# Matrix memory's scores and numerators as three fp32r products each, in a two-layer mixer block

## The reference

```
s[t,u]  = (q[t] . k[u]) * exp(decay of gates from u to t)      u before or at t
num[t]  = sum_u s[t,u] * v[u]
den[t]  = sum_u s[t,u]
h[t]    = num[t] / max(|den[t]|, exp(-m[t]))
```

## Time and profile before

| | us |
|---|---|
| three runs | 2364.0, 2364.7, 2366.33; median 2364.7 |
| profiled execution | 2365.41 |
| its span | 2363.6 |

### The profile page before, as it was taken

The page is one execution under the profiler, slowest core; times in us unless marked ns, Lnnn a source line. Parts: engine busy times, 40 slices in busy tenths (PEclk is TensorE's granted clock), DMA queues, the critical chain, the costliest instruction groups (busy, mean ns, idle before and its releaser), DMA issues.

```text
span 2363.6 us, 35388 instructions
## 1 busy us (share of the span) xinstructions
PE 2334.6 (99%) x12814; PEld 2023.9 (86%) x12814; DVE 1633.9 (69%) x2731; ACT 1012.8 (43%) x1721; POOL 196.2 (8%) x186
## 2 busy tenths in 40 slices
PE   8999999999999999999999999999999999999998
PEld 5888889887888888898888898888898898999997
DVE  6998577455547655569885368886665656778876
ACT  5422224435346544363222264222245346666554
POOL 2111000000000000021210000111100000001220
PEclk9999999999999999999999999999999999999999
DMA  8787464332222332337783328775534433556654
GB/s 277 245 253 240 126 207 143 82 97 72 72 63 81 90 89 68 111 90 244 239 249 113 95 77 252 239 233 181 172 110 125 109 106 103 156 144 196 192 162 136
DMA packets 540056, 356.87 MB, mean 151 GB/s; under 512 B 15206, under 2 KB 490896, under 8 KB 539920
## 3 DMA queue, kind: packets, MB, share of 16 engines
q1 hardware_dynamic: 538472, 354.70, 51.0%
q10 hardware_dynamic: 1448, 0.38, 0.1%
HBM read 337.20 MB, written 17.83 MB: 150 GB/s over the span
## 4 chain that ended last, share of the span: by engine, by line
PE 89%; DVE 4%; ACT 2%; issue 2%; DMA 1%; SPq 1%; POOL 0%; DVEq 0%; ACTq 0%; POOLq 0%
PE ps L1054 24%; PE ps L1056 24%; PE ps L1055 24%; PE ps L1419 2%; PE ps L1352 2%; PE ps L1353 2%; PE ps L1354 2%; PE ps L1067 1%; DVE w_lo L2249 1%; PE ps L1146 1%; PE ps L1147 1%; PE ps L1148 1%; PE ps L1395 1%; PE ps L1452 1%; PE ps L1069 1%
## 5 line engine op out<-in xcount | busy, mean ns | idle before, releaser
L2249 DVE TENSOR_TENSOR w_lo<-raw,w_hi 128x1024 fp32r<-128x1024 f32 (+3 forms) x430 | 497.7, 1158 | 444.9 <-ACT w_hi L1558 440.7
L1558 ACT ACTIVATE w_hi<-raw 128x1024 fp32r<-128x1024 f32 (+3 forms) x430 | 423.3, 985 | 849.1 <-PE ps L1056 673.5
L1054 PE MATMUL ps<-u_hi,w_hi 128*128 128x512 f32 (+2 forms) x2176 | 782.7, 360 | 1.0 <-DVE w_lo L2249 0.7
L1056 PE MATMUL ps<-u_hi,w_lo 128*128 128x512 f32 (+2 forms) x2176 | 773.0, 355 | 0.0
L1055 PE MATMUL ps<-u_lo,w_hi 128*128 128x512 f32 (+2 forms) x2176 | 772.8, 355 | 0.0
L1054 PEld LDWEIGHTS ps<-u_hi,w_hi 128*128 128x128 f32 x2176 | 411.5, 189 | 60.0 <-issue 1.4
L1056 PEld LDWEIGHTS ps<-u_hi,w_lo 128*128 128x128 f32 x2176 | 411.3, 189 | 58.3
L1055 PEld LDWEIGHTS ps<-u_lo,w_hi 128*128 128x128 f32 x2176 | 411.6, 189 | 55.7
L2667 DVE SCALAR_TENSOR_TENSOR ada_acc<-ada_in_up,cs,ada_acc 128x512 f32<-128x512 f32 x378 | 279.1, 800 | 0.0
L1054 PE MATMUL ps<-g,w_hi 128*128 128x512 f32 (+1 forms) x572 | 206.7, 361 | 0.0
L1056 PE MATMUL ps<-g,w_lo 128*128 128x512 f32 (+1 forms) x572 | 203.8, 356 | 0.0
(11 more groups left out here) (346 smaller groups left out, 3562.3 us busy)
## 6 DMA issues: line engine op xcount, KB each, us to landing
raw<-in_ffn_up SPq DMA_DIRECT2D x150, 512.0 KB, 4.6
raw<-in_w_in SPq DMA_DIRECT2D x132, 512.0 KB, 3.7
ada_in_up<-in_w_ada SPq DMA_DIRECT2D x108, 512.0 KB, 4.4
raw<-in_ffn_down SPq DMA_DIRECT2D x67, 384.0 KB, 3.2
fold_out<-ada_acc SPq DMA_DIRECT2D x32, 512.0 KB, 3.2
fold<-fold_out SPq DMA_DIRECT2D x32, 512.0 KB, 5.5
raw<-in_ffn_down SPq DMA_DIRECT2D x42, 320.0 KB, 3.1
h<-in_ffn_up SPq DMA_DIRECT2D x22, 512.0 KB, 4.6
```

The costliest lines, as they stand in the source:

```text
L1054: pe.matmul(ps[bank][:, cols_of], wh, a_hi, start=a, stop=False)
L1056: m = pe.matmul(ps[bank][:, cols_of], wl, a_hi, start=False, stop=b)
L1558: act.activation(hi, whole, ACT.Copy).then_inc(hi_done, 1)
L2249: dve.tensor_tensor(lo, whole, hi.bitcast(F32), ALU.subtract).then_inc(lo_done, 1)
```

## The change

The scores of the memory become three fp32r products each, from rounded and remaining parts of queries and keys; so do the numerators, now of 258 columns (the last is zero, for an even number), from rounded and remaining parts of weights and values. New steps on ScalarE and VectorE make these parts: `ml_v` for a head's values (before its scores), `ml_p` for its weights (behind its scores), `qk_high` and `qk_low` for the next head's queries and keys. TensorE waits for the last of nine subtractions (`pv_split`) instead of the eight blocks of `pw`. The rounded weights lie in unused parts of `pw` and in places free at that time.

In layer 1's gate stage the first scores come one chunk later, and queries are split for a whole head at once, ahead of the squares. Layer 0's last `da` chunk has its z split before the weight split of the same step. Not shown are the new tiles and semaphores, a zero written to column 257, the calls of the new steps from each engine's loop, and the shifted place of odd heads' queries in `qs`.

```diff
@@ -182,6 +182,8 @@
         order.append(("mk", n) if n < 4 else ("mv", n - 4))
+        if n in (6, 8):
+            order.append(("qk_high" if n == 6 else "qk_low", 0))
         if n in GATES_BEHIND:
@@ -191,9 +193,10 @@
     for h in range(HEADS):
-        order += [("ml_s", h, s) for s in range(TT)] + fill[0:2]
-        order += [("ml_n", h, 0), ("ml_n", h, 1)] + fill[2:3]
+        order += [("ml_v", h)] + [("ml_s", h, s) for s in range(TT)] + [("ml_p", h)] + fill[0:2]
+        order += [("ml_n", h, 0), ("ml_n", h, 1)] + fill[2:3] + [("qk_high", h + 1)] * (h + 1 < HEADS)
         order += [("ml_h", h, 0), ("ml_n", h, 2), ("ml_h", h, 1), ("ml_n", h, 3)] + fill[3:4]
+        order += [("qk_low", h + 1)] * (h + 1 < HEADS)
         order += [("ml_h", h, 2), ("ml_h", h, 3), ("ml_t", h)] + fill[4:5]
@@ -210,7 +213,7 @@
             s3 = order.index(("ml_s", h, 3))
-            order[s3], order[s3 + 1] = order[s3 + 1], order[s3]
+            order[s3:s3 + 3] = order[s3 + 2:s3 + 3] + order[s3:s3 + 2]
         elif vector:
@@ -255,10 +258,14 @@
         first = 4 * (head - 1)
-        for t in range(units_of_head(layer)):
-            at = first + 2 * KD // len(attention_units(layer)[0]) * t
-            parts.setdefault(at, []).append(("q_high", head, t))
-            parts.setdefault(at + 1, []).append(("q_low", head, t))
+        if layer == DEPTH - 1:
+            steps = {0: ("q_high", head), 1: ("q_low", head), 2: ("k_high", head), 3: ("k_low", head)}
+            if p - first in steps:
+                return [steps[p - first]]
+            continue
+        for t in range(TT):
+            parts.setdefault(first + t, []).append(("q_high", head, t))
+            parts.setdefault(first + t + 1, []).append(("q_low", head, t))
         parts.setdefault(first + 1, []).append(("k_high", head))
@@ -274,12 +281,17 @@
             order += [("turn", v - 1), ("scores", v)]
+        if p == 1 and every == 2:
+            order.append(("scores", 0))
         if every == 2 and p == 2 * KD - 1:
...
         order.append(("sc", p) if p < KD else ("ml", p - KD))
-        if p % every == 0:
+        if every == 2:
+            order += head_parts(layer, p)
+        if p % every == 0 and (v or every == 1):
             order.append(("outputs", v - 1) if v else ("scores", 0))
-        order += head_parts(layer, p)
+        if every == 1:
+            order += head_parts(layer, p)
     last = [("outputs", units - 1), ("rms", 0)]
@@ -470,7 +483,10 @@
     yml_lo = at("yml_lo", [P, 8, TOK], F32R, region + 32 * KB)
-    vaug = at("vaug", [P, TT, HEADS, 257], F32, region + 16 * KB)
+    vaug = at("vaug", [P, TT, HEADS, 258], F32, region + 16 * KB)
+    vaug_low = at("vaug_low", [P, TT, HEADS, 258], F32R, region + 16 * KB)
+    vaug_hi = at("vaug_hi", [P, TT, 258], F32R, 1152 + 3 * KB)
+    pw_b3 = at("pw_b3", [P, SEG], F32R, 1152 + 2 * KB)
     neg_g = at("neg_g", [P, TOK], F32R, region + 32 * KB + KB // 2)
@@ -697,9 +720,29 @@
         t0, n = t0_of(layer), units_of_head(layer)
-        if head == 0:
-            return slice(t0, TOK), 16 * layer + n, n
+        if head == 0 or layer == DEPTH - 1:
+            return slice(t0, TOK), 16 * layer + n * (head + 1), n
         return slice(t0 + t * P, t0 + (t + 1) * P), 16 * layer + n * head + t + 1, 1
+
+    def query_place(layer, head):
+
+        return t0_of(layer) if layer == DEPTH - 1 and head % 2 else 0
+
+    def pw_hi(n, s, b, e):
+
+        if n == 0 and s == 0:
+            return ada_round[:, b:e]
+        if n == 0:
+            return pw_low[:, 0, TT - s, b - s * P:e - s * P]
+        if s == 0:
+            return pw_low[:, 1, 3, b - SEG:e - SEG] if b >= SEG else pw_low[:, 1, 2, b:e]
+        if s == 1:
+            return low_round[:, b:e]
+        return pw_low[:, 1, 2, b - P:e - P] if s == 2 else pw_b3[:, b - SEG:e - SEG]
+
+    def ml_rounded(head):
+
+        return (qk_hi[:, head, 0, :], qk_hi[:, head, 1, :]) if head else (ada_round, low_round)
@@ -1385,15 +1428,16 @@
-                base, a0, d0 = BASES[layer, "proj"]
-                pe.wait_ge(evac_act, a0 + PLANS[layer]["mq", head][2] + 1)
-                pe.wait_ge(evac_dve, d0 + PLANS[layer]["mk", head][3] + 1)
+                pe.wait_ge(qk_ready, u + 1)
                 wait(pe, hsum_ready, nth_out(layer, head, 0))
...
             ts = max(t0, SEG if s >= 2 else 0)
-            pe.matmul(ps[SCORE_ML[s]][:, ts:TOK], kt[:, head, s * P:(s + 1) * P], qt[:, head, ts:TOK],
-                      start=True, stop=True).then_inc(s_ready, 1)
+            out, keys = ps[SCORE_ML[s]][:, ts:TOK], slice(s * P, (s + 1) * P)
+            q_hi, k_hi = ml_rounded(head)
+            pe.matmul(out, k_hi[:, keys], q_hi[:, ts:TOK], start=True, stop=False)
+            pe.matmul(out, k_hi[:, keys], qt_low[:, head, ts:TOK], start=False, stop=False)
+            pe.matmul(out, kt_low[:, head, keys], q_hi[:, ts:TOK], start=False, stop=True).then_inc(s_ready, 1)
@@ -1410,14 +1454,18 @@
             u = HEADS * layer + head
-            pe.wait_ge(pw_ready, 8 * (u + 1))
+            pe.wait_ge(pv_split, 9 * (u + 1))
             if t > first + 1:
                 pe.wait_ge(hsum_ready, nth_out(layer, head, t) - 1)
+            own = slice(t * P, (t + 1) * P)
             for n, w in enumerate("fb"):
                 keys = KEYS[w, t]
+                out = ps[NUMERATOR[t % 2][n]][:, 0:258]
                 for s in keys:
-                    m = pe.matmul(ps[NUMERATOR[t % 2][n]][:, 0:257], pw[:, n, s, t * P:(t + 1) * P], vaug[:, s, head, :],
-                                  start=(s == keys[0]), stop=(s == keys[-1]))
+                    rounded = pw_hi(n, s, t * P, (t + 1) * P)
+                    pe.matmul(out, rounded, vaug_hi[:, s, :], start=(s == keys[0]), stop=False)
+                    pe.matmul(out, rounded, vaug_low[:, s, head, :], start=False, stop=False)
+                    m = pe.matmul(out, pw_low[:, n, s, own], vaug_hi[:, s, :], start=False, stop=(s == keys[-1]))
             m.then_inc(num_ready, 1)
@@ -1921,18 +1969,51 @@
+        def ml_values(layer, head):
+
+            act.wait_ge(evac_dve, BASES[layer, "proj"][2] + PLANS[layer]["mv", 7][3] + 1)
+            if head:
+                act.wait_ge(num_ready, nth_out(layer, head, t0_of(layer) // P))
+            act.activation(vaug_hi[:, :, :], vaug[:, :, head, :], ACT.Copy).then_inc(pv_high, 1)
+
+        def ml_weights(layer, head):
+
+            act.wait_ge(s_ready, TT * (HEADS * layer + head + 1))
+            for s in range(TT):
+                for n in range(2):
+                    act.wait_ge(pw_ready, 8 * (HEADS * layer + head) + 2 * s + n + 1)
+                    for b, e in segments(s, n, t0_of(layer))[0]:
+                        m = act.activation(pw_hi(n, s, b, e), pw[:, n, s, b:e], ACT.Copy)
+                    m.then_inc(pv_high, 1)
+
+        def ml_high(layer, head):
+
+            base, a0, d0 = BASES[layer, "proj"]
+            t = slice(t0_of(layer), TOK)
+            act.wait_ge(evac_act, a0 + PLANS[layer]["mq", head][2] + 1)
+            if head == 0:
+                act.wait_ge(ada_turned, (ADA_OF[1, "up0"] if layer else ADA_OF[0, "up1"]) - 4 +
+                            (ADA_UP + ADA_DOWN[1] if layer else 0))
+            q_hi, k_hi = ml_rounded(head)
+            act.activation(q_hi[:, t], qt[:, head, t], ACT.Copy)
+            act.wait_ge(evac_dve, d0 + PLANS[layer]["mk", head][3] + 1)
+            act.activation(k_hi[:, :], kt[:, head, :], ACT.Copy).then_inc(qk_high, 1)
+
         def queries_high(layer, head, t=None):
             cols_of, done, n = query_tiles(layer, head, t)
+            place = slice(cols_of.start - query_place(layer, head), cols_of.stop - query_place(layer, head))
             act.wait_ge(rope_done, 8 * layer + 2 * (head + 1))
-            if head:
+            if layer == DEPTH - 1 and head >= 2:
+                act.wait_ge(sc_ready, 2 * (done - 2 * units_of_head(layer)))
+            elif head and layer < DEPTH - 1:
                 act.wait_ge(sc_ready, 2 * (done - units_of_head(layer)))
-            else:
+            elif head == 0:
                 act.wait_ge(ada_turned, (ADA_OF[1, "up0"] if layer else ADA_OF[0, "up1"]) - 4 +
...
                 for rows_of in HALF_ROWS:
-                    m = act.activation(qs[rows_of, j, 0, cols_of], dqk[own, head, cols_of], ACT.Copy)
+                    m = act.activation(qs[rows_of, j, 0, place], dqk[own, head, cols_of], ACT.Copy)
             m.then_inc(q_high, n)
@@ -1995,6 +2076,10 @@
             n, t0 = GATE_CHUNKS[layer].index(step), t0_of(layer)
+            z_first = step == ("da", KD - 1) and layer < DEPTH - 1
+            if z_first:
+                act.wait_ge(z_sum, KD * layer + k + 1)
+                act.activation(z_hi[:, k, t0:TOK], gate_temp(step)[:, t0:TOK], ACT.Copy).then_inc(z_hi_done, 1)
             ahead(base, n, kn=(GATE_CHUNKS[layer] + [("gs", 0)] * 4)[n + SPLIT][0] in ("sc", "da") and 4 or KD)
@@ -2014,7 +2099,7 @@
```

(38 more changed lines are left out.)

19 lines of the change are left out of this document (18 added, 1 removed).

## The result

| | before | after |
|---|---|---|
| median, us | 2364.64 (2363.14 to 2367.65, 20 runs) | 2369.19 (2366.42 to 2371.56, 20 runs) |
| ratio | | 1.0017, 95% interval 1.0011 to 1.0023 |
| profiled execution, us (its span) | 2365.41 (2363.6) | 2366.91 (2365.1) |

I had forecast 2363, a gain of 1.6. The measured loss is smaller than the 0.2% (4.7 us) that I called the limit of a measurement, yet its sign is settled: the interval excludes 1, three times.

What follows compares the result with a forecast made beforehand. TensorE, its matmuls filling 99% of the span, was taken as the bound. The terms -13.6 + 5.6 + 11.4 - 1.4 - 3.4 = -1.4 took the profiled 2365.4 to 2364.0, median 2363; range 2355 to 2370.

Steps and rivals of the forecast that it cites:

- TensorE's saving: Memory scores and numerators of both layers as three fp32r products: 8.1 saved in layer 0, 5.5 in layer 1, together 13.6.
- Waits at the numerators, evacuation, sum: New TensorE waits in the memory's heads for rounding on ScalarE and VectorE: 5.6 lost in layer 0, 11.4 in layer 1.
- z: Layer 0's last gate chunk: z split before the weight split removes TensorE's wait for z_lo, gain 1.4.
- The copies hide: Rival, memory heads: copies run closer or in idle time, half of the 17 us of waits gone, 2354.5; chance 0.30.
- Weight loads bind: Rival, numerators: three weight loads of 0.19 instead of two passes count, costing 28 us, 2391; chance 0.01.
- The clock falls in layer 1's memory: Rival: waits ahead of layer 1's numerators reach 2 us, each costing 1.7 more, 2369.8; chance 0.21, longer waits included.
- The attention part: Layer 1's gate stage: reordered scores and query splits gain 0.8 and 3.8, late keys_low loses 2 x 0.6; net -3.4.
- keys_low of heads 2 and 3: Layer 1's attention: split keys stand behind a full weight split on VectorE, 2 x 0.6 lost.
- The rest of that term: Layer 1's attention: 0.8 from scores one chunk later, 3.8 from earlier turned weights and no clock fall.
- ks_even's 1.6: Layer 1's attention: TensorE's 1.6 wait for ks_even goes as scores move one chunk back; bounds 0 and 1.6, 0.8 taken.
- The fourth rival: Attention part keeps its waits or new ones replace them: 2366.7; no own chance, part of the forecast's case (0.48).

Runs made afterwards that it cites:

- e2: The kernel before with the z edit alone (layer 0's last gate chunk splits z ahead of the weight split): 2363.37 us, ratio 0.9996.
- e5: The change with the rounding of a head's values placed half a head earlier: 2359.64 us, ratio 0.9979.
- e4: The change with layer 1's k_low (heads 1 to 3) moved up to right behind the outputs: 2362.85 us, ratio 0.9992.
- e10: The change with ScalarE's squares in layer 1 held until behind the next chunk's weight copy: 2365.77 us, ratio 1.0003.
- e1: The change again, no edit: 2368.18 us, ratio 1.0017 to the kernel before.
- e3: The change with layer 1's attention order and query splits as in the kernel before: 2366.65 us, ratio 1.0012.
- e9: The change once more, no edit, timed beside e10: 2368.10 us, ratio 1.0017 to the kernel before.
- e6: The change with both placements, those of e4 and e5 together: 2352.96 us, ratio 0.9956.
- e7: As e6, with the weights' rounding cut per key tile and set between the scores' steps: 2351.42 us, ratio 0.9946.
- e8: As e4, with the memory's numerators as fp32 products again, without rounding of values or weights: 2356.56 us, ratio 0.9968.
- e11: e7 again, no edit: 2350.29 us, ratio 0.9938 to the kernel before.
- e12: As e11, with layer 1's numerators in fp32, without their rounding steps; layer 0 keeps three products: 2348.76 us, ratio 0.9935.

## Why the prediction was wrong

- **TensorE's saving, 13.6.** Right. Numerators 0.075 each in layer 0, (6.07 - 5.05) / 14 = 0.073 in layer 1 (forecast 0.071); scores 0.47 and some 0.3 a head (forecast 0.60 and 0.38). About 13.2. The 110 ns that I set against the rows are what the Trainium skill (TensorE: Matmul & The Clock Gate, Back-to-back issue gap) gives for a single product by itself; the rows are streams of products with a weight load each, so they don't contradict it.
- **Waits at the numerators, evacuation, sum: 17.0.** Right: 16.9, term by term. The serial count on VectorE and ScalarE was enough; the overlap between consecutive operations was worth only 0.1 each.
- **z: -1.4.** Right: -1.3 (e2).
- **The copies hide** (my first rival, 0.30): refuted; no wait was smaller than counted by more than 0.1. e5 shows what it would have taken, another place.
- **Weight loads bind**: refuted, 0.119 a product with a load each.
- **The clock falls in layer 1's memory**: not seen. The time of this rival, 2369.8, lies beside the measured 2369.2 and the upper end of my range, 2370, was there for its sake; that the number falls inside the range is luck. In three profiles of the change every window over layer 1's heads has the clock at 1.00. Two of after's, the second behind the wait of 2.20 and over that of 2.07 (stretch, its length, TensorE's busy time, granted clock, DMA share, GB/s):

```profile
1892.00:1918.00 26.00, 24.04 (x178) 1.00 0.30 82
...
2025.00:2050.00 25.00, 22.93 (x186) 1.00 0.62 172
```

- **The attention part, -3.4: here the prediction failed**, at the sentence "keys_low of heads 2 and 3 now stands behind a full weight split (1.06 + 1.22 + 1.39 behind the chunk's end, wanted 3.2 behind it): 2 x 0.6 lost". Three heads wait, not two: 2.20, 2.07 and 0.60 in the rows; by e4 they cost 5.3 where I had 1.2, a loss of 4.1 more. The last one is the 0.6 of the forecast. For the other two the chain that I summed began at the chunk's end, with one split ahead of the keys, and assumed that VectorE and ScalarE come to it on time. They don't. The chunk in front has only four key tiles there (1.44 of TensorE), so the split of the chunk before it is still to be done, and an evacuation: in the rows the keys end 5.5 behind the chunk's end (2018.23 to 2023.77) where I had 3.67. And the squares, which the change leaves between the key copy and the weight copy, wait for VectorE's oda, and ScalarE's lateness comes back to VectorE as 1.42 of idle time. I had used that very coupling for the gain ("before the squares, which wait for VectorE") and not for the loss. e10 removes this part and gets 2.3 back; that the rest is the second split is read off the rows and not tested.
- The rest of that term was nearly right: without the keys the attention gains 5.3 - 1.5 = 3.8, where I had 0.8 + 3.8 = 4.6. The turn's new wait of 0.9 leaves 0.7 of ks_even's 1.6 (forecast 0.8).
- **The fourth rival**, that the attention's gain is replaced by new waits (2366.7), was the case that came, only larger. I had put it inside the forecast and did not look for its price.

In medians of the first group: memory and z +2.0 (forecast +2.0), attention +1.5 (forecast -3.4), together +3.5. The first measurement stands 1 us higher still, 2369.19 against 2368.18 and 2368.10 for the same kernel. The executions of the three overlap (2366.42 to 2371.56 and 2366.55 to 2369.75 in the first two), so this may be scatter; no run explains it.

## What to carry to other kernels

Rounding operands for shorter products moves work from the full engine to two idle ones, but each of these works in order: the cost is set by what the new step stands in front of, not by how full the engine is. Moving one step of 2.3 us (eight times) half a head forward was worth 8.5 us, and moving one of 1.4 us (three times), 5.3. When a step is moved ahead of a wanted operand, follow the chain back over both engines until it reaches something that is surely on time; a sum from the last event of TensorE is a lower bound. Where a stage leaves the two engines little room, look at it head by head: in layer 1 one head lost 3.0 and those behind it gained 0.2 to 0.4, and the longer product was the better choice there only because of that one.

## What the runs showed that I had not expected

**A wait costs more than the trace's bracket says**, 0.26 us with products of 256 to 512 columns; over 16 such waits that is 4 us, as much as the whole difference measured here (3.4 to 4.55).

**Executions of kernels with a wait over 2 us more often have a lower mean clock.** The mean granted clock over the execution is listed to three places. Of the kernels with one or more waits of 2.1 to 2.2 on TensorE in layer 1's attention (after, e1, e2, e3, e5, e9, and before in the three groups) 51 of 145 executions show 0.999, the others 0.998 or 0.997. Of those without one (e4, e6, e7, e8, e10, e11, e12) 43 of 48 do. e10, whose only edit shortens two waits from 2.2 and 2.1 to 1.15 and 1.04, has 10 of 11, e9 beside it 5 of 11. Within a kernel the executions at 0.998 take longer, by 1.7 in after, 0.8 in e1 and 1.5 in e9 (means). A profile shows one execution: the wait of 2.1 for wgt_t ended in a fall in two of three profiles (before and e3, 0.72 and 0.74 in six us, and not in e2), the waits of 2.2 and 2.1 for the keys in none of four (after, e1, e9, e5). That these waits are the cause is therefore not shown. Two other things vary from execution to execution. The clock also falls at the very end of all fourteen profiles, and not equally: its mean over the last 12 us is 0.82 in after, 0.70 in e1, and e1's profile shows 0.998 with no other fall. And TensorE's wait for fold near 106 us is 0.3 in e1, 0.5 in before and 2.1 in e8. So the lower clock goes with the kernels that have the waits, but where it falls in the executions that were not profiled stays open, and so does why after's median lies up to 2.3 us above its profiled execution.
